# Block compression with its matmul sides swapped, in a one-core transformer kernel

## The chip, the cores and the metric

The kernel runs on one NeuronCore of a Trainium2 chip. The metric is the device time of one execution in microseconds (us). Three executions of the kernel before took 2712.67 to 2714.38 us, median 2713.49 us.

## The reference

The program is two transformer blocks over 512 positions of width 1024. The change touches one small part of the first block, the compression of keys and values for the sparse attention:

```python
def compress(kv, pe, w1, w2):
    """NSA compression phi: (B,S,G,hd) -> (B,Nc,G,hd); block i covers [i*STRIDE, i*STRIDE+CMP_BLOCK)."""
    ...
    blocks = blocks + pe[None, None, :, None, :]
    n_cmp = blocks.shape[1]
    flat = blocks.transpose(0, 1, 3, 2, 4).reshape(b, n_cmp, g, CMP_BLOCK * d)
    return jax.nn.silu(flat @ w1) @ w2

    k_cmp = rmsnorm(compress(kc, cmp_pe_k, cmp_w1_k, cmp_w2_k), k_norm_g)
    v_cmp = compress(vc, cmp_pe_v, cmp_w1_v, cmp_w2_v)
```

A block is 32 positions of 64 features, 2048 numbers; blocks start every 16 positions, so there are 31 of them for each of 4 groups, 124 in all. `w1` is 2048 x 256, `w2` is 256 x 64. It is done twice, for keys (q = 0) and for values (q = 1).

## The kernel before, in words

**Precision.** Nearly every product is made from numbers split in two: a high part rounded to `F32R` and the low rest. For a weight unit of 128 x 1024 numbers, ScalarE copies the high part (`split` in `act_program`, through `copy`, L1324), VectorE subtracts it from the raw weights (L1702), and TensorE makes three products, high x high, high x low, low x high (`three`, L870). All matmuls that are not transposes are recorded at L868.

**Order.** `order()` writes one list of items; each engine's program walks through that list and issues its share, so each engine's queue holds the items in the same order. Weight units are numbered as they are added; the split of unit n+1 is issued on ScalarE and VectorE just ahead of the item that uses unit n, into one of two buffers, and waits until TensorE has finished unit n-1. SyncE loads up to three units ahead.

**The stage.** `memory_branch` runs the attention over the memory (four heads of four tiles), and fills its waits with other work. `attend` (L279) adds for each tile a `score`, a `turn` of the tile three back, and two steps of the jobs. The jobs take turns: one is `wide` (L270), the queries of the next head: two dense units, then `widestat` (sum of squares by TensorE, then a chain of small VectorE and ScalarE operations, `rsqrt`, L1713), then `widefin` (TensorE spreads the result, VectorE scales both halves, ScalarE and VectorE split them). The next head's first `score` waits for that split. The other job is `compress()` (L402), then `queries` and `keys`.

**The compression.** `kvc` makes the projection (a dense unit), VectorE writes it to `C2`, feature by position, with the next position's features in the lower 64 partitions. `cmp(q, j)` handles weight unit j of 4 (four slabs of 128 x 256). Its weights are not split: `split=False`, the raw fp32 slab is the stationary side, in halves of 128 columns, and `C2` moves, 124 columns that lie 16 numbers (64 bytes) apart. A second matmul with one moving column adds the position encoding's part into another column of the bank. An fp32 matmul shows in the trace as two. After j = 3 VectorE copies that column to `hb` and ScalarE writes `hid` = silu(bank + hb), hidden unit by block, which `kc1` and `vc` multiply by `w2`.

Of the kernel before, what the change touches and what calls it, by code (L numbers as in the profile page):

```python
# [14 lines left out]
P = 128  # L15
# [200 lines left out]
def order():  # L216
# [461 lines left out]
def build(nc, A, out):  # L678
# [44 lines left out]
    hid = [place(f"hid{q}", 24576 + q * 256, 256).rearrange("p (t g c) -> p t g c", t=2, g=4) for q in range(2)]  # L723
    KX = place("KX", 25088, 128)
# [47 lines left out]
    hb = sb("hb", [P, 4])  # L772
# [90 lines left out]
    def pe_program(e):  # L863
# [230 lines left out]
        def cmp(q, j, n):  # L1094
            if j == 0:
                for ht in range(2):
                    take("d", ("cmp", q, ht), True)
                on.wait_ge(*evac.at(("c2", q, 1)))
            bs = [banks[("cmp", q, ht)] for ht in range(2)]
            on.wait_ge(*d_raw[n % NRAW].at(n))  # L1100
            for kk in range(4):
                kt = 4 * j + kk
                for ht in range(2):
# [4 lines left out]
            f.then_inc(*full.tick(("u", n), *([("cmp", q)] if j == 3 else [])))  # L1108
            if j == 3:
                for ht in range(2):  # L1110
                    banks.let_go(("cmp", q, ht))

        def kc1():
            b = take("d", ("kc1",))
            on.wait_ge(*d_w2.at(0))
            on.wait_ge(*curve.at(("hid", 0, 1)))
# [8 lines left out]
        def vc():  # L1125
            b = take("d", ("vc",))
            on.wait_ge(*curve.at(("hid", 1, 1)))
# [171 lines left out]
        def mmo(m, n):  # L1299
# [4 lines left out]
            for k in range(2):  # L1304
# [6 lines left out]
                  turn=turn, values=values, rel=rel, kvc=kvc, cmp=cmp, kc1=kc1, kc2=kc2, vc=vc, ng=ng, gn=gnt, sq=sq,  # L1311
# [8 lines left out]
    def act_program(e):  # L1320
# [143 lines left out]
        def cmp(q, j, n):  # L1464
            for ht in range(2 if j == 3 else 0):
                on.wait_ge(*evac.at(("hb", q, ht)))
                o = banks[("cmp", q, ht)][:, 0:124].rearrange("p (g c) -> p g c", g=4)
                on.wait_ge(*cleared.at("hid"))
# [972 lines left out]
```

## Time and profile before

| | us |
|---|---|
| median of three runs | 2713.49 |
| profiled execution | 2708.38 |
| its span, first to last instruction | 2706.6 |
| TensorE busy | 2544.7 (94%) |
| VectorE busy | 1350.9 (50%) |
| ScalarE busy | 1042.8 (39%) |
| mean granted TensorE clock | 0.963 of full |

Busy time is the time in which an engine has an instruction running. Loads of TensorE's stationary side (PEld) overlap its matmuls (PE). The names of buffers lose their numbers, so `C2` is `t_C` and `w_qm` units appear as `t_raw`, `t_whi`, `t_wlo`.

### The profile page before, as it was taken

Reading aid. Unit: us, or ns where it says so; the run is one execution under the profiler, and the core shown is the slowest. Engines: PE = TensorE matmul, PEld = TensorE weight load, DVE = VectorE, ACT = ScalarE, POOL = GpSimd, SP = SyncE. Lnnn points to the kernel's source line nnn. Section 1 sums busy time; section 2 is a strip of 40 time slices with the busy share of each in tenths; the row PEclk is TensorE's granted clock in tenths of the full one; section 3 lists DMA queues with packets and bytes.
Section 4 is the critical chain, followed back from the end, with each engine's and each line's share of the span. In section 5 each row is a group of like instructions: output and inputs, shape, how many; then the busy total and the mean of one; then the engine's idle time right before and its main releaser. Section 6 shows DMA issues by size and latency. Waiting matters only on the chain.

```text
span 2706.6 us, 31528 instructions
## 1 busy us (share of the span) xinstructions
PE 2544.7 (94%) x12154; PEld 2113.1 (78%) x12154; DVE 1350.9 (50%) x2707; ACT 1042.8 (39%) x1865; POOL 175.9 (6%) x236
## 2 busy tenths in 40 slices
PE   8989998899999999999999999999989988899998
PEld 6867887788788787877888887877878776688886
DVE  5424445433466656666543444655544455543444
ACT  4213334333454454444332233655542345322222
POOL 0000000000011111111000000111100002000000
PEclk9999998898899899999999999999989999999999
DMA  3473234122212111212223223211112331223222
GB/s 131 101 142 109 91 103 149 60 72 71 70 67 74 48 63 51 75 55 102 87 94 100 95 88 124 78 55 55 55 47 93 106 120 55 70 93 94 101 87 85
DMA packets 85982, 231.38 MB, mean 85 GB/s; under 512 B 8344, under 2 KB 23320, under 8 KB 85834
## 3 DMA queue, kind: packets, MB, share of 16 engines
q1 hardware_dynamic: 78480, 217.18, 24.1%
q10 hardware_dynamic: 7354, 12.19, 2.4%
q8 instruction: 98, 1.61, 0.3%
q14 instruction: 50, 0.41, 0.0%
HBM read 217.79 MB, written 11.53 MB: 85 GB/s over the span
## 4 chain that ended last, share of the span: by engine, by line
PE 81%; DVE 9%; ACT 5%; issue 2%; DMA 2%; POOL 1%; ACTq 1%; DVEq 0%; SPq 0%
PE bank L868 79%; DVE t_wlo L1702 2%; PE bank L1035 2%; DMA t_raw<-in_f_out 1%; ACT t_whi L1324 1%; DVE t_tmp L1774 1%; DVE t_ss L1903 0%; POOL t_pp L2257 0%; DVE t_CB L1774 0%; POOL t_pw L2259 0%; DVE t_tmp L1744 0%; ACT t_pp L1451 0%; DVE t_ST L2152 0%; ACTq L1392 0%; DVE t_tmp L1782 0%
## 5 line engine op out<-in xcount | busy, mean ns | idle before, releaser
L868 PE MATMUL bank<-t_XH,t_whi 128*128 128x512 f32 x2064 | 829.2, 402 | 53.8 <-DVE t_wlo L1702 24.8
L868 PE MATMUL bank<-t_XH,t_wlo 128*128 128x512 f32 x2064 | 815.8, 395 | 0.0
L868 PE MATMUL bank<-t_XL,t_whi 128*128 128x512 f32 x2064 | 815.6, 395 | 0.0
L1702 DVE TENSOR_TENSOR t_wlo<-t_raw,t_whi 128x1024 fp32r<-128x1024 f32 (+2 forms) x412 | 472.0, 1147 | 480.1 <-ACT t_whi L1324 475.2
L1324 ACT ACTIVATE t_whi<-t_raw 128x1024 fp32r<-128x1024 f32 (+2 forms) x412 | 407.2, 989 | 410.3 <-PE bank L868 361.9
L868 PEld LDWEIGHTS bank<-t_XH,t_whi 128*128 128x128 f32 x2064 | 396.2, 192 | 150.2 <-issue 42.3
L868 PEld LDWEIGHTS bank<-t_XH,t_wlo 128*128 128x128 f32 x2064 | 394.6, 191 | 85.1
L868 PEld LDWEIGHTS bank<-t_XL,t_whi 128*128 128x128 f32 x2064 | 395.7, 192 | 79.2
L868 PE MATMUL bank<-t_RX,t_whi 128*128 128x512 f32 x1056 | 334.1, 398 | 11.5 <-DVE t_wlo L1702 6.6
L868 PEld LDWEIGHTS bank<-t_RX,t_whi 128*128 128x128 f32 x1056 | 200.0, 190 | 60.5 <-ACT t_whi L1324 7.0
L1774 DVE TENSOR_TENSOR t_tmp<-bank,t_RB 128x512 f32<-128x512 f32 x170 | 117.0, 688 | 259.1 <-PE bank L868 256.1
L868 PE MATMUL bank<-t_RX,t_wlo 128*128 128x512 f32 x528 | 210.0, 398 | 0.0
L2259 POOL TENSOR_SCALAR t_pw<-t_pw,t_sa 128x256 f32<-128x256 f32 (+1 forms) x80 | 68.5, 859 | 984.8 <-DVE t_sa L1916 983.8
L1324 ACT ACTIVATE t_RX<-t_tmp 128x512 fp32r<-128x512 f32 x66 | 41.7, 632 | 223.6 <-DVE t_tmp L1782 223.6
L868 PEld LDWEIGHTS bank<-t_RX,t_wlo 128*128 128x128 f32 x528 | 99.9, 189 | 24.3
L2257 POOL TENSOR_SCALAR t_pp<-t_pp,t_sa,t_gn 128x128 f32<-128x128 f32 (+3 forms) x128 | 86.0, 672 | 412.4 <-DVE t_sa L1916 412.4
L1451 ACT ACTIVATE t_pp<-t_ss,t_sa 128x256 f32<-128x256 f32 (+3 forms) x144 | 79.8, 554 | 76.5 <-DVE t_sa L1903 74.9
L1385 ACT ACTIVATE t_tmp<-t_tmp 128x512 f32<-128x512 f32 x66 | 41.7, 632 | 133.9 <-DVE t_tmp L1774 133.9
L1035 PE MATMUL bank<-t_cst,t_pp 128*128 128x128 f32 x352 | 66.6, 287 | 19.9 <-POOL t_pp L2257 19.9
L1324 ACT ACTIVATE t_PS<-bank 128x128 fp32r<-128x128 f32 (+3 forms) x128 | 54.7, 427 | 79.0 <-PE bank L1035 78.7
L868 PE MATMUL bank<-t_OA,t_whi 128*128 128x512 f32 x256 | 81.9, 402 | 3.1 <-ACT t_OA L1324 3.1
L1324 ACT ACTIVATE t_XH<-t_XT,t_vec 128x512 fp32r<-128x512 f32 x48 | 34.6, 721 | 123.2 <-DVE t_XT L2078 57.9
(300 smaller groups left out, 2882.5 us busy)
## 6 DMA issues: line engine op xcount, KB each, us to landing
t_raw<-in_f_in SPq DMA_DIRECT2D x88, 512.0 KB, 3.2
t_raw<-in_f_out SPq DMA_DIRECT2D x32, 384.0 KB, 3.1
t_raw<-in_w_merge SPq DMA_DIRECT2D x24, 512.0 KB, 3.2
t_raw<-in_w_conv SPq DMA_DIRECT2D x24, 512.0 KB, 3.2
t_raw<-in_fg SPq DMA_DIRECT2D x22, 512.0 KB, 3.2
t_raw<-in_fu SPq DMA_DIRECT2D x22, 512.0 KB, 3.2
t_raw<-in_f_out SPq DMA_DIRECT2D x32, 320.0 KB, 2.9
t_raw<-in_w_g SPq DMA_DIRECT2D x16, 512.0 KB, 3.3
```

Of the source, the lines that this page charges most:

```text
L868: return e.matmul(o, l, r, start=start, stop=stop, skip_group_check=True)
L1035: f = e.transpose(b[:, j * P:(j + 1) * P], spare(hd, t)[1][:, j * P:(j + 1) * P], ident)
L1324: return e.activation(o, i, ACT.Copy, **how)
L1385: e.activation(s, a, ACT.Silu).then_inc(*curve.tick(("silu", f, h, m)))
L1451: e.activation(p[:, 0:wd], x[:, 0:wd], ACT.Exp, scale=-1.0, bias=s[:, 0:1], accum_out=s[:, 1:2]).then_inc(*curve.tick(("ex", t)))
L1702: e.tensor_tensor(wlo[n % NW][:, 0:width], raw[n % NRAW][:, 0:width], f32(whi[n % NW][:, 0:width]), ALU.subtract).then_inc(*w_lo.tick(n))
L1774: e.tensor_tensor(o, banks[item], RB, ALU.mult).then_inc(*evac.tick(done, ("free", item)))
L2257: e.tensor_scalar(p, p, r, gn[:, i, k:k + 1], ALU.mult, ALU.mult).then_inc(*scaled.tick(t))
L2259: e.tensor_scalar(p, p, r, None, ALU.mult).then_inc(*scaled.tick(t))
```

## The change

The sides of the compression's matmul are swapped, the position encoding is added before the matmul, and both sides are split.

- `cround(q, j)`, new, on VectorE: four `tensor_scalar` write the high part of C2's strided columns plus the position encoding, into `CH[0][j % 2]` (124 numbers wide, one for each of four slabs); then four `scalar_tensor_tensor` write the low part into `CH[1][j % 2]`.
- `cmp(q, j)` on TensorE: the 124 columns of `CH` are the stationary side, the split weights (256 columns, contiguous) move: 4 slabs x 3 products = 12 `F32R` matmuls, into one bank, block by hidden unit. Its unit is split as all others.
- ScalarE applies silu to the whole bank at once into `HS`; `hturn(q)`, new, turns `HS` back by two transposes on TensorE, and VectorE copies them to `hid`.
- `compress()` has one more step for each q: the first of them holds only a `cround`, and `cmp(q, 3)` stands by itself ahead of `hturn`. The copies to `hb` go.

```diff
             for j in range(4):
-                w.lin("cmp", q, j, name="cmp_w1", j=4 * q + j, split=False)
+                w.add("cround", q, j)
+                if j:
+                    w.lin("cmp", q, j - 1, name="cmp_w1", j=4 * q + j - 1)
                 yield
+            w.lin("cmp", q, 3, name="cmp_w1", j=4 * q + 3)
+            yield
+            w.add("hturn", q)
...
         def cmp(q, j, n):
...
-            for kk in range(4):
-                kt = 4 * j + kk
-                for ht in range(2):
-                    l = raw[n % NRAW][:, kk * 256 + ht * P:kk * 256 + (ht + 1) * P]
-                    o = bs[ht][:, 0:124].rearrange("p (g c) -> p g c", g=4)
-                    mm(o, l, C2[:, :, 2 * kt:2 * kt + 481:16], kt == 0, kt == 15)
-                    f = mm(bs[ht][:, 126:127], l, v(("pek", "pev")[q], kt), False, kt == 15)
+            b = take("d", ("cmp", q), True) if j == 0 else banks[("cmp", q)]
+            hi, lo = weights(n)
+            on.wait_ge(*x_lo.at(("cround", q, j)))
+            h, l = CH[0][j % 2], CH[1][j % 2]
+            for kk in range(4):
+                c = slice(kk * 256, (kk + 1) * 256)
+                f = three(b[0:124, 0:256], h[:, kk, 0:124], l[:, kk, 0:124], hi[:, c], lo[:, c],
+                          j == 0 and kk == 0, j == 3 and kk == 3)
...
+        def hturn(q):
+            b = take("d", ("hturn", q))
+            on.wait_ge(*curve.at(("hs", q)))
+            for ht in range(2):
+                f = e.transpose(b[:, ht * P:ht * P + 124], HS[0:124, ht * P:(ht + 1) * P], ident[0:124, 0:124])
+            f.then_inc(*full.tick(("hturn", q)))
...
         def cmp(q, j, n):
...
+            if j == 3:
+                on.wait_ge(*full.at(("cmp", q, 3)))
+                on.wait_ge(*full.at(("hturn", q - 1)))
+                e.activation(HS[0:124, :], banks[("cmp", q)][0:124, 0:256], ACT.Silu).then_inc(
+                    *curve.tick(("hs", q), ("free", ("cmp", q))))
...
+        def cround(q, j):
+            h, l = CH[0][j % 2], CH[1][j % 2]
+            on.wait_ge(*evac.at(("c2", q, 1)))
+            on.wait_ge(*full.at(("cmp", q, j - 2) if j > 1 else ("cmp", q - 1, j + 2)))
+            src = [C2[:, :, 2 * kt:2 * kt + 481:16] for kt in range(4 * j, 4 * j + 4)]
+            for kk in range(4):
+                o = h[:, kk, 0:124].rearrange("p (g c) -> p g c", g=4)
+                e.tensor_scalar(o, src[kk], v(("pek", "pev")[q], 4 * j + kk), None, ALU.add).then_inc(*calc.tick(("cround", q, j)))
+            on.wait_ge(*calc.at(("cround", q, j)))
+            for kk in range(4):
+                o, i = (x[:, kk, 0:124].rearrange("p (g c) -> p g c", g=4) for x in (l, h))
+                e.scalar_tensor_tensor(o, src[kk], v(("pek", "pev")[q], 4 * j + kk), f32(i), ALU.add, ALU.subtract).then_inc(
+                    *x_lo.tick(("cround", q, j)))
```

## Rows read from the trace of the kernel before

**Rows 1.** The profile page: TensorE, clock in 40 slices, chain by line.
```profile
PE 2544.7 (94%) x12154; PEld 2113.1 (78%) x12154; DVE 1350.9 (50%) x2707; ACT 1042.8 (39%) x1865; POOL 175.9 (6%) x236
...
PEclk9999998898899899999999999999989999999999
...
PE bank L868 79%; DVE t_wlo L1702 2%; PE bank L1035 2%; DMA t_raw<-in_f_out 1%; ACT t_whi L1324 1%; DVE t_tmp L1774 1%; DVE t_ss L1903 0%; POOL t_pp L2257 0%; DVE t_CB L1774 0%; POOL t_pw L2259 0%; DVE t_tmp L1744 0%; ACT t_pp L1451 0%; DVE t_ST L2152 0%; ACTq L1392 0%; DVE t_tmp L1782 0%
```

**Rows 2.** Windows, the eight compression blocks: busy by engine, clock, DMA share.
```profile
523.41:530.12 6.71, 6.71 (x35) 6.71 (x34) 1.17 (x7) 0.51 (x2) 0.00 (x0) 0.54 0.00 0
...
548.02:552.98 4.96, 4.96 (x34) 4.91 (x32) 1.23 (x1) 2.12 (x3) 0.00 (x0) 1.00 0.00 0
...
sum 44.21, PE 44.21 PEld 43.95 DVE 12.97 ACT 16.52 POOL 0.00; mean PE 5.53 PEld 5.49 DVE 1.62 ACT 2.06 POOL 0.00
```

**Rows 3.** Windows, the whole stage, then a slow and a fast stretch of one unit.
```profile
518.00:668.00 150.00, 141.60 (x704) 126.73 (x704) 53.39 (x122) 49.92 (x85) 10.51 (x12) 0.86 0.20 71
...
539.00:544.60 5.60, 5.60 (x19) 4.78 (x20) 1.45 (x5) 0.87 (x3) 0.92 (x1) 0.52 0.51 187
544.60:548.00 3.40, 3.40 (x16) 2.80 (x15) 0.00 (x0) 0.00 (x0) 0.00 (x0) 1.00 0.00 0
```

**Rows 4.** Waits of TensorE from 500 to 760 us: total, times, longest.
```profile
PE bank L868 <- DVE t_tmp L1843: 6.4, 3, 3.4
PE bank L868 <- DVE t_wlo L1702: 4.7, 5, 3.0
```

**Rows 5.** Timeline of TensorE: start, duration, instruction, idle before it.
```profile
506.20 0.88 PE L868 MATMUL bank<-t_MK,t_MQ 128*128 128x256 f32 x6
506.92 0.39 PE L868 MATMUL bank<-t_XH,t_whi 128*128 128x512 f32 x1
...
522.50 1.05 PE L868 MATMUL bank<-t_cst,t_tmp 128*128 128x1 f32 x8 [3.35 <-DVE t_tmp L1843]
...
531.96 1.91 PE L868 MATMUL bank<-t_cst,t_sn 128*128 128x128 f32 x8
...
539.00 1.63 PE L868 MATMUL bank<-t_MK,t_MQ 128*128 128x256 f32 x6
540.43 0.63 PE L1035 MATMUL bank<-t_cst,t_pp 128*128 128x128 f32 x2
540.71 0.78 PE L868 MATMUL bank<-t_XH,t_whi 128*128 128x512 f32 x1
...
567.12 1.05 PE L868 MATMUL bank<-t_cst,t_tmp 128*128 128x1 f32 x8 [1.53 <-DVE t_tmp L1843]
```

**Rows 6.** Timeline of VectorE.
```profile
525.04 0.16 DVE L1736 SCALAR_TENSOR_TENSOR t_sn<-t_sn,t_rn 128x4 f32<-128x4 f32 x1
...
533.91 0.69 DVE L1854 TENSOR_TENSOR t_wq<-t_wq,bank 128x512 f32<-128x512 f32 x1 [0.87 <-PE bank L868]
...
537.42 0.69 DVE L1707 TENSOR_TENSOR t_MQ<-t_wq,t_MQ 128x512 fp32r<-128x512 f32 x1 [0.77 <-ACT t_MQ L1324]
...
659.06 0.69 DVE L1822 SCALAR_TENSOR_TENSOR t_XT<-t_mg,bank 128x512 f32<-128x512 f32 x1 [0.68 <-PE bank L868]
```

**Rows 7.** Groups of VectorE, shapes apart: busy us, mean ns of one.
```profile
L1702 DVE TENSOR_TENSOR t_wlo<-t_raw,t_whi 128x1024 fp32r<-128x1024 f32 x316 | 386.5, 1224 | 340.7 <-ACT t_whi L1324 338.4
...
L1711 DVE SCALAR_TENSOR_TENSOR t_XL<-t_XT,t_vec,t_XH 128x512 fp32r<-128x512 f32 x48 | 36.0, 750 | 31.7 <-ACT t_XH L1324 31.7
...
L1707 DVE TENSOR_TENSOR t_PS<-bank,t_PS 128x128 fp32r<-128x128 f32 x32 | 8.7, 273 | 0.6 <-ACT t_PS L1324 0.4
...
L2039 DVE TENSOR_TENSOR t_tmp<-bank,t_TB 128x31 f32<-128x31 f32 x16 | 2.1, 195 | 0.0
...
L2039 DVE TENSOR_TENSOR t_tmp<-bank,t_TB 128x15 f32<-128x15 f32 x16 | 1.7, 169 | 0.0
```

**Rows 8.** Groups of ScalarE, shapes apart: the split of a unit.
```profile
L1324 ACT ACTIVATE t_whi<-t_raw 128x1024 fp32r<-128x1024 f32 x316 | 331.6, 1050 | 218.0 <-PE bank L868 201.4 <-issue 9.4 <-DMA t_raw<-in_f_in 4.5
```

**Rows 9.** Groups of TensorE's stationary loads, shapes apart.
```profile
L868 PEld LDWEIGHTS bank<-t_XH,t_whi 128*128 128x128 f32 x2064 | 396.2, 192 | 150.2 <-issue 42.3 <-DVE t_sa L1903 7.8 <-ACT t_whi L1324 7.7
```

More of the change, by code:

```diff
@@ L723, in build @@
     hid = [place(f"hid{q}", 24576 + q * 256, 256).rearrange("p (t g c) -> p t g c", t=2, g=4) for q in range(2)]
+    CH = [[place(f"CH{q}{d}", 25728 + 1024 * q + 512 * d, 512, F32R).rearrange("p (k n) -> p k n", k=4) for d in range(2)]
+          for q in range(2)]
+    HS = place("HS", 27776, 256)
     KX = place("KX", 25088, 128)
@@ L771, in build @@
     vch = sb("vch", [P, 64], F32R)
-    hb = sb("hb", [P, 4])
     csm = sb("csm", [P, 4, 4, 4])
@@ L1115, in kc1 @@
             on.wait_ge(*d_w2.at(0))
-            on.wait_ge(*curve.at(("hid", 0, 1)))
+            on.wait_ge(*evac.at(("hid", 0)))
             mm(b[:, 0:P], w2s[:, 0:P], hk[0], True, False)
@@ L1126, in vc @@
             b = take("d", ("vc",))
-            on.wait_ge(*curve.at(("hid", 1, 1)))
+            on.wait_ge(*evac.at(("hid", 1)))
             mm(b[:, 0:64], hk[2], w2s[:, 256:320], True, False)
@@ L1310, in pe_program @@
                   convg=convg, wide=wide, widestat=widestat, widefin=widefin, memv=memv, mgate=mgate, score=score,
-                  turn=turn, values=values, rel=rel, kvc=kvc, cmp=cmp, kc1=kc1, kc2=kc2, vc=vc, ng=ng, gn=gnt, sq=sq,
+                  turn=turn, values=values, rel=rel, kvc=kvc, cmp=cmp, hturn=hturn, kc1=kc1, kc2=kc2, vc=vc, ng=ng, gn=gnt, sq=sq,
                   sqstat=sqstat, sqfin=sqfin, sk=sk, skstat=skstat, skfin=skfin, sv=sv, cscore=cscore, cnorm=cnorm, cturn=cturn,
@@ L1464, in cmp @@
         def cmp(q, j, n):
[L1465 to L1468, printed above, removed]
-                e.activation(hid[q][:, ht, :, 0:31], o, ACT.Silu, bias=hb[:, 2 * q + ht:2 * q + ht + 1]).then_inc(
-                    *curve.tick(("hid", q, ht), ("free", ("cmp", q, ht))))
+            if j == 3:
[3 more added lines that the diff above has]
+                    *curve.tick(("hs", q), ("free", ("cmp", q))))
         def scaled_sq(b, sq, x, gain, sq_item, x_item, free):
@@ L1937, in kvc, with hturn @@
                     *evac.tick(("c2", q, x), ("free", ("kvc", q, x))))
-        def cmp(q, j, n):
-            if j == 3:
-                on.wait_ge(*full.at(("cmp", q)))
-                for ht in range(2):
-                    e.tensor_copy(hb[:, 2 * q + ht:2 * q + ht + 1], banks[("cmp", q, ht)][:, 126:127]).then_inc(
-                        *evac.tick(("hb", q, ht)))
+        def cround(q, j):
[11 more added lines that the diff above has]
+                    *x_lo.tick(("cround", q, j)))
+        def hturn(q):
+            on.wait_ge(*full.at(("hturn", q)))
+            on.wait_ge(*cleared.at("hid"))
+            src = banks[("hturn", q)][:, 0:256].rearrange("p (t n) -> p t n", t=2)
+            for ht in range(2):
+                e.tensor_copy(hid[q][:, ht, :, 0:31], src[:, ht, 0:124].rearrange("p (g c) -> p g c", g=4)).then_inc(
+                    *evac.tick(("hid", q), ("free", ("hturn", q))))
         def kc2():
@@ L2232, in dve_program @@
                   gateu=gateu, mmerge=mmerge, smerge=smerge, gmerge=gmerge, weigh=weigh, scale=scale, rest=rest,
-                  rel=rel, kvc=kvc, cmp=cmp, kc2=kc2, vc=vc, ng=ng, gn=gnt, sqstat=sqstat, sqfin=sqfin,
+                  rel=rel, kvc=kvc, cround=cround, hturn=hturn, kc2=kc2, vc=vc, ng=ng, gn=gnt, sqstat=sqstat, sqfin=sqfin,
                   skstat=skstat, skfin=skfin, skput=skput, svs=svs, csoft=csoft, cnorm=cnorm, cturn=cturn, msplit=msplit, po=po,
```

11 lines of the change are left out of this document (2 added, 9 removed).

## The prediction, before the run

> **What bounds the kernel now.** I read the page first. TensorE is busy 94% of the span, the chain that ended last lies on its matmuls for 79%, and the clock row dips below 9 in a few slices [rows 1]. So work taken off TensorE shortens the run, unless something it covered comes to light. The windows over the whole stage, 518 to 668 us, come next: TensorE 141.6 of 150 us, VectorE 53.4, ScalarE 49.9, mean clock 0.86 [rows 3]. VectorE has room on average; what counts is where its chains end. TensorE's waits say that: from 500 to 760 us it waits 6.4 us in three waits for the sum ahead of `widestat` (L1843) and 4.7 us for split weights [rows 4]. Everything else the small chains need is covered, and much of the cover is the compression.
>
> **What goes.** The windows over the eight `cmp` blocks: 4.96 us at full clock (1.00), up to 6.71 us where the clock is near its lower level of 1.2 GHz (0.54), 44.2 us in all, with TensorE busy throughout [rows 2]. The two pairs of copies to `hb` and the halves of the silu had their own short place beside other work; I put them at nothing either way, since silu, now one instruction, and its table loads stay.
>
> **What comes on TensorE.** Eight times 12 matmuls with 256 moving columns. The trace has six such (`score`): they start at 506.20 and the next matmul at 506.92, 0.12 us each; at the lower clock 539.00 to 540.43, 0.24 us each [rows 5]. A `cmp` block is then 1.44 us, or 2.86 us. TensorE's idle times ahead of `widestat` are what precede the slow stretches [rows 2, 3, 5], and three of the eight blocks follow such a wait at once; I take 3 x 2.86 + 5 x 1.44 = 15.8 us. Four transposes: two at the lower clock take 0.28 us (540.43 to 540.71) [rows 5], so about 0.6 us. Net work: 44.2 - 15.8 - 0.6 = 27.8 us less.
>
> The stationary side has 124 columns instead of 128. A stationary load lasts 192 ns [rows 9], longer than the 120 ns from one matmul to the next: the loads overlap, and I assume they go on doing so. If they didn't, a matmul would cost 0.19 us, 96 x 0.07 = 7 us more.
>
> **What comes on VectorE.** Eight splits more, 1.22 us each [rows 7], after 1.05 us on ScalarE [rows 8]: 9.8 and 8.4 us. Eight `cround` of eight instructions. Bounds for one instruction: from below 0.195 us (31 columns taken 16 apart); from above 0.75 us (the same kind of operation, 512 columns) [rows 7]. A contiguous 128 columns take 0.273 us. The strided reads cost (195 - 169)/16 = 1.6 ns a column, against (1224 - 273)/896 = 1.06 for contiguous ones, which puts 124 strided columns at 195 + 93 x 1.6 = 0.34 us [rows 7]. The writes here are contiguous and half the instructions have one tensor input. I take 0.31 us, 2.5 us for a `cround` (1.6 to 6.0), 20 us for the eight. The Trainium skill, SBUF — State Buffer, Door 1: The DMA port swizzle, says that SBUF has 16-byte lines and each access that crosses to a new line pays a penalty. The slope of 1.6 against 1.06 ns agrees; by contiguous rates alone a `cround` would be 2.2 us, and the sum below about 2 us better.
>
> VectorE in the stage goes from 53 to about 81 us, in some 136 us: still not the bound on average. DMA moves the same bytes and raw buffers come free sooner, after the split and not after the matmuls; nothing there.
>
> **Where the cover was.** This is the larger half of the working. I walked through the items. `compress()` gets two steps more, so everything behind its first `cround` moves: kvc(1,0) comes after `widefin` of head 2, kvc(1,1) goes beside the queries of head 3, cmp(1,2) and cmp(1,3) behind the values of head 1. Four places lose cover, with c = 2.5 for a `cround`:
>
> (a) Head 1's queries. Before: `widestat` at 522.50, cmp(0,0), `score`, `turn`, `widefin`, cmp(0,1), `score` at 539.00, the next dense unit at 540.71 [rows 5]. After: `widestat`, `score`, `turn`, `widefin`, cmp(0,0), `score`. The `rsqrt` chain ends at 525.2 [rows 6], so `widefin`, eight matmuls at the lower clock (531.96 to about 533.7 before [rows 5]), runs until 527.0. VectorE does `cround`(0,0) from 525.2 to 527.7: cmp(0,0) waits 0.7 and ends at 530.6. VectorE then has `weigh` and `rest` (about 1.0 us) and the query chain, which took 533.91 to 538.11 = 4.2 us [rows 6]: 532.9. `score` waits 2.3. Then on VectorE `cround`(0,1), 2.5, and the next unit's split, 1.2: 536.7, while TensorE has finished at 534.7: 2.0 more. Waits of 5.0 us, and the dense unit starts at 536.7 instead of 540.71.
>
> (b) `widestat` of head 2. Before it idled 1.53 us behind cmp(0,3) [rows 5]. With cmp(0,2) of 1.44 us and a split behind `cround`(0,3) ahead of the sum on VectorE, I get 2.5 us: 1.0 more.
>
> (c) Head 3's queries, where cmp(1,0) and cmp(1,1) cover less. Counting from `widestat`'s start: `widefin` at 5.6, VectorE has `cround`(1,1) and a split until 6.8, `weigh`, `rest` to 7.8, the query chain to 12.0, `cround`(1,2) and a split to 15.7. TensorE is ready for `score` at 8.6 to 10.0 and for the gate unit at 13.4: about 2.3 + 2.2 = 4.5.
>
> (d) cmp(1,3). The values of head 1 end at V; VectorE merges until V + 0.7 (it waited for them until 659.06, then 0.69 us [rows 6]), then `cround`(1,3) to V + 3.2 and the split to V + 4.4. cmp(1,2) is done at V + 1.4: 3.0 us. `hturn` is covered by `score` and `turn`.
>
> Together 13.5 us. Behind the stage, `sqfin` now stands after two gate units and loses a wait of under 1 us, while `skstat` loses its neighbours; I leave these at zero. Stretches at the lower clock outside the `cmp` blocks: 19 instructions in 5.60 us at 0.52 against 16 in 3.40 at 1.00 [rows 3] put one at about 1.6 us. The number of them seems the same after as before, with up to three more possible at the new waits; zero, with 5 us kept for the range.
>
> **The sum.** 27.8 - 13.5 = 14 us less. The profiled execution took 2708.38 us (span 2706.6 and 1.8 around it), so 2694.4; it lies 5.1 us below the median of the three runs, 2713.49. On that scale I predict **2699.5 us**, own range 2693 to 2706.
>
> **The rivals.**
>
> *Nearly all of the 27.8 us is kept.* `cround` is short (1.6 us) or the clock stays up. For it: VectorE is busy only 53 of 150 us. Against: it is the order of its queue, not its load, that makes the waits. At c = 1.6 six `cround` lie on the path of (a) to (d), 6 x 0.9 = 5.4 better, and with one slow stretch less 7: 2692.5; with no waits at all 2685.7. Chance 0.19.
>
> *The 124-column load is not hidden.* 0.19 us a matmul, 7 us more, 2706.5. For it: 192 ns against 120 [rows 9, 5]. Against: full-width loads of that length are hidden throughout, 2064 times. The Trainium skill, TensorE: Matmul & The Clock Gate, Weight-path perf modes, gives fast weight load only for 128 weights and no FP32; if `F32R` has it now, the change loses it, with the result of this case. Chance 0.10.
>
> *The waits eat it all.* The slow stretches multiply: each new wait of over 2 us, four of them, followed by a stretch that costs 1.6, plus (b) and the tail once more: 6 + 5 us, 2710.5. For it: before, the idle of 3.35 us was followed by a clock of 0.54 [rows 5, 2]. Chance 0.10.
>
> *VectorE decides, slower than before.* If strided instructions with two steps cost as much as 512 columns, 0.75 us, a `cround` is 6.0 us; the six on the path add 6 x 3.5 = 21: 14 - 21, 7 us slower, 2720.5. It turns at c = 2.5 + 14/6 = 4.8 us, 0.60 us an instruction. Against: 31 strided columns take 0.195 us. Chance 0.06.
>
> The forecast itself has 0.55.
>
> **How the numbers follow.** About 0.2% (5.4 us) can be told from no change here. The forecast and the first two rivals are all below 2708: 0.55 + 0.19 + 0.10 = 0.84 faster, less a little for their edges, 0.83. The third is half within 0.2%, and edges of others: 0.09 same. The rest, 0.08, slower. The range reaches from the first rival, 2687, to the third, 2710.
>
> **What would show each step.** `cmp` groups of 256 columns with starts 0.12 us apart; a wider spacing shows the load. `cround` groups near 0.31 us an instruction. TensorE's waits between 518 and 650 us: about 20 us in all, for t_MQ at the first `score` of heads 1 and 3, for t_wlo right behind it, for t_tmp (L1843) at `widestat`, for t_wlo at cmp(1,3). The gate unit of head 0 about 13 us earlier than before; the stage's mean clock not below 0.84. The prediction is wrong if these waits are under 8 or over 25 us, or if the gain appears outside the stage.

## The result and the profile after

The changed kernel takes 2698.43 us (median of four runs, 2693.39 to 2702.08); the kernel before, timed beside it, 2713.14. The ratio is 0.9946, 95% interval 0.9931 to 0.9962: 14.7 us faster, where 14 were forecast. Two later groups of runs gave 0.9953 (0.9934 to 0.9971) and 0.9949 (0.9929 to 0.9968). The profiled execution took 2702.08 us with a span of 2700.3; it is the slowest of its four, so its span understates the gain.

The page of the kernel after, its lines that answer to [rows 1]: 156 matmuls fewer, TensorE busy 27.9 us less, 31 us more on VectorE.

```profile
PE 2516.8 (93%) x11998; PEld 2082.8 (77%) x11998; DVE 1381.6 (51%) x2779; ACT 1051.0 (39%) x1870; POOL 176.5 (7%) x236
...
PEclk9999999898989999999999999999989999999999
...
PE bank L875 77%; DVE t_wlo L1709 2%; PE bank L1042 2%; ACT t_whi L1332 1%; DMA t_raw<-in_f_out 1%; DVE t_tmp L1781 1%; DVE t_ss L1910 1%; POOL t_pp L2279 0%; DVE t_CB L1781 0%; ACT t_pp L1459 0%; ACT t_tmp L1332 0%; POOL t_pw L2281 0%; DVE
```

Windows over three of the eight compression blocks, the answer to [rows 2]; all eight add up to 15.25 us of TensorE's time (forecast 15.8), where 44.21 stood. The number before the last two of a row is the granted clock: two of the eight blocks run at the lower clock (0.50), two more in part.

```profile
526.58:529.37 2.79, 2.79 (x13) 2.62 (x13) 2.02 (x7) 1.24 (x3) 0.92 (x1) 0.50 0.00 0
542.95:544.39 1.44, 1.44 (x13) 1.44 (x12) 0.00 (x0) 1.24 (x3) 0.00 (x0) 1.00 0.00 0
...
...
641.63:643.54 1.91, 1.91 (x13) 1.91 (x14) 1.03 (x1) 0.00 (x0) 0.00 (x0) 0.75 0.52 124
```

To compare the rest I cut both traces at the same items: from the first `score` of the memory attention (491.20 before, 490.00 after) to the first matmul of `kc1` (the product of `hid` with `w2`, the first item behind the compression), and from there to `sv`, the first weight unit of the values for the sparse attention. Between the two lie, among others, `skfin`, which spreads the norms of the sparse keys, and `skput`, which splits and stores them. The window views, before and then after; the third line of the second is the stretch of [rows 3].

```profile
491.20:664.30 173.10, 163.77 (x786) 144.43 (x787) 59.88 (x129) 56.65 (x93) 11.44 (x12) 0.87 0.20 70
664.30:741.80 77.50, 70.10 (x357) 57.63 (x355) 34.12 (x68) 36.75 (x58) 4.55 (x5) 0.89 0.16 55
```

```profile
490.00:651.30 161.30, 135.87 (x639) 115.07 (x639) 88.56 (x205) 63.94 (x101) 12.39 (x13) 0.88 0.22 72
651.30:727.80 76.50, 66.35 (x349) 54.84 (x347) 33.11 (x61) 31.99 (x51) 8.14 (x7) 0.91 0.23 76
518.00:668.00 150.00, 122.67 (x587) 104.70 (x588) 86.86 (x210) 65.16 (x106) 13.31 (x14) 0.87 0.21 71
```

In the first stretch, the stage from here on, TensorE is busy 163.77 us before and 135.87 after: 27.9 less. It is idle 9.3 us before and 161.30 - 135.87 = 25.4 after: 16.1 more. The stage is 11.8 us shorter. In the second stretch the idle time goes from 7.4 to 10.2, the busy time falls by 3.8, and 1.0 us more is gained.

The waits of TensorE from 500 to 760 us, against [rows 4], and the timeline of TensorE with the idle time ahead of each, against [rows 5]:

```profile
PE bank L875 <- DVE t_wlo L1709: 17.6, 9, 3.2
PE bank L875 <- DVE t_tmp L1850: 8.8, 3, 3.3
PE bank L875 <- DVE t_sn L1743: 4.8, 2, 4.3
PE bank L875 <- DVE t_MQ L1714: 3.8, 3, 1.5
```

```profile
521.32 1.05 PE L875 MATMUL bank<-t_cst,t_tmp 128*128 128x1 f32 x8 [3.35 <-DVE t_tmp L1850]
...
531.42 0.59 PE L875 MATMUL bank<-t_MK,t_MQ 128*128 128x256 f32 x3 [1.20 <-DVE t_MQ L1714]
...
534.95 0.77 PE L875 MATMUL bank<-t_XH,t_whi 128*128 128x512 f32 x1 [2.71 <-DVE t_wlo L1709]
...
546.68 0.47 PE L875 MATMUL bank<-t_XH,t_whi 128*128 128x512 f32 x1 [1.19 <-DVE t_wlo L1709]
...
557.41 1.86 PE L875 MATMUL bank<-t_cst,t_tmp 128*128 128x1 f32 x8 [2.63 <-DVE t_tmp L1850]
...
606.73 1.05 PE L875 MATMUL bank<-t_cst,t_tmp 128*128 128x1 f32 x8 [2.84 <-DVE t_tmp L1850]
...
621.52 0.77 PE L875 MATMUL bank<-t_XH,t_whi 128*128 128x512 f32 x1 [2.72 <-DVE t_wlo L1709]
...
641.63 0.35 PE L875 MATMUL bank<-t_whi,t_CH 128*124 128x256 f32 x1 [2.92 <-DVE t_wlo L1709]
...
724.19 3.68 PE L875 MATMUL bank<-t_cst,t_sn 128*64 128x128 f32 x32 [4.29 <-DVE t_sn L1743]
...
737.00 0.36 PE L875 MATMUL bank<-t_whi,t_XH 128*128 128x256 f32 x1 [3.15 <-DVE t_wlo L1709]
```

The place names of the prediction are, in this order: `widestat` of head 1; (a) the second half of head 1's queries and the dense unit behind them; a dense unit two items later; (b) `widestat` of head 2; `widestat` of head 3; (c) the gate unit (a dense weight unit for the output gate) behind head 3's queries; (d) cmp(1,3). The last two lie behind the stage: `skfin`, and the second `sv` unit.

### The profile page after: what moved, and what is told of

Read it like the earlier page. It is cut to its first block, busy times and chain, and to the rows that moved or that the text cites. A ratio compares the mean times of both kernels' runs of the same rounds, so it can differ in the third digit from the quotient of the medians.

```text
span 2700.3 us, 31304 instructions
## 1 busy us (share of the span) xinstructions
PE 2516.8 (93%) x11998; PEld 2082.8 (77%) x11998; DVE 1381.6 (51%) x2779; ACT 1051.0 (39%) x1870; POOL 176.5 (7%) x236
## 4 chain that ended last, share of the span: by engine, by line
PE 78%; DVE 10%; ACT 6%; issue 3%; DMA 2%; POOL 1%; ACTq 1%; DVEq 0%; SPq 0%
PE bank L875 77%; DVE t_wlo L1709 2%; PE bank L1042 2%; ACT t_whi L1332 1%; DMA t_raw<-in_f_out 1%; DVE t_tmp L1781 1%; DVE t_ss L1910 1%; POOL t_pp L2279 0%; DVE t_CB L1781 0%; ACT t_pp L1459 0%; ACT t_tmp L1332 0%; POOL t_pw L2281 0%; DVE t_tmp L1751 0%; DVE t_ST L2174 0%; ACTq L1400 0%
## 5 line engine op out<-in xcount | busy, mean ns | idle before, releaser
L1709 DVE TENSOR_TENSOR t_wlo<-t_raw,t_whi 128x1024 fp32r<-128x1024 f32 (+2 forms) x420 | 482.0, 1149 | 480.7 <-ACT t_whi L1332 476.1
L1332 ACT ACTIVATE t_whi<-t_raw 128x1024 fp32r<-128x1024 f32 (+2 forms) x420 | 416.1, 992 | 409.5 <-PE bank L875 360.8
L875 PE MATMUL bank<-t_RX,t_whi 128*128 128x512 f32 x1056 | 333.8, 397 | 11.8 <-DVE t_wlo L1709 6.9
```

The lines of the kernel that those rows point to most:

```text
L875: return e.matmul(o, l, r, start=start, stop=stop, skip_group_check=True)
L1332: return e.activation(o, i, ACT.Copy, **how)
L1709: e.tensor_tensor(wlo[n % NW][:, 0:width], raw[n % NRAW][:, 0:width], f32(whi[n % NW][:, 0:width]), ALU.subtract).then_inc(*w_lo.tick(n))
```

## The experiments

Times are medians; each ratio is to the kernel before on the same chip, with its 95% interval. The kernel before ran at 2708.86 us in the first group (30 runs, 2700.27 to 2719.05), 2713.03 in the second and 2711.65 in the third. "Stage" is the stretch from the first `score` to `kc1`, "first values" the time from the first `score` to the first matmul with the sparse values; both are read in one profiled execution, to about 0.1 us. Three profiles of the changed kernel (after, e0_again, e11_control) differ by 1.3 us in the stage and by 2.9 us at the first values, so smaller differences of single profiles say nothing. Where runs of different groups are compared, go by the ratios.

| | median us | ratio | stage | first values |
|---|---|---|---|---|
| before (profile) | 2713.14 | 1 | 173.1 | 287.1 |
| after | 2698.43 | 0.9946 | 161.3 | 280.0 |
| e0_again | 2692.91 | 0.9953 [0.9934, 0.9971] | 162.2 | 278.4 |
| e1_order_only | 2718.90 | 1.0035 [1.0019, 1.0051] | 173.1 | 290.9 |
| e2_old_steps | 2703.85 | 0.9976 [0.9961, 0.9991] | 162.2 | 279.7 |
| e3_round_twice | 2716.48 | 1.0035 [1.0021, 1.0049] | 178.4 | 297.2 |
| e4_swap | 2693.22 | 0.9942 [0.9923, 0.9960] | 158.6 | 274.7 |
| e5_pairs | 2702.80 | 0.9969 [0.9956, 0.9983] | (other order) | 284.2 |
| e6_few_rounds | 2691.87 | 0.9924 [0.9910, 0.9939] | 155.1 | 271.1 |
| e7_high_on_act | 2694.41 | 0.9940 [0.9925, 0.9955] | 157.5 | 276.2 |
| e8_zero_later | 2692.52 | 0.9930 [0.9909, 0.9951] | 158.2 | 273.4 |
| e9_early_third | 2688.85 | 0.9915 [0.9894, 0.9936] | 153.5 | 271.2 |
| e10_both | 2687.09 | 0.9914 [0.9892, 0.9935] | 153.6 | 270.4 |
| e11_control | 2697.01 | 0.9949 [0.9929, 0.9968] | 161.0 | 277.1 |

**e0_again**, the changed kernel once more, as the measure for the first group.

> The changed kernel once more, with five rounds. Theory (the gain is 28 to 29 us of matmuls less, minus about 15 us of waits that appear where the compression was the cover): 12 to 16 us below the kernel before. It also shows how far its executions spread; the first four went from 2693.4 to 2702.1, and if that is the clock's state at the waits, a second profile should show the same waits in the stage and a different length behind it.

0.9953; its waits lie where those of the first profile lie (`widestat` 3.36, 2.63 and 2.85, units 2.73, 1.20 and 2.44, cmp(1,3) 2.94). The places are a property of the order, not of one execution.

**e1_order_only**, the kernel before with the item order of the change and nothing else:

```diff
             for j in range(4):
-                w.lin("cmp", q, j, name="cmp_w1", j=4 * q + j, split=False)
+                if j:
+                    w.lin("cmp", q, j - 1, name="cmp_w1", j=4 * q + j - 1, split=False)
                 yield
+            w.lin("cmp", q, 3, name="cmp_w1", j=4 * q + 3, split=False)
+            yield
```

> The kernel before with nothing but the new order of steps (two more steps, each cmp one step later; raw weights, old matmuls). Theory: the order itself costs, behind the stage, where the norms of the queries and keys lose their neighbours (in the changed kernel TensorE waits 4.3 us for the key statistics and 3.2 us for the split of the second value unit, which the kernel before did not): 3 to 6 us slower than before, with the stage itself about as long. Rival A: the order is free (within 2 us) and those waits come from the rounding and the splits on VectorE. Rival B: the order gains, because compression blocks now lie beside other chains: faster by over 2 us.

The order alone makes the kernel 0.35% slower. The stage is not the cause (173.1 us, as before); the loss stands behind it. Timeline of TensorE in e1_order_only, `skfin` and the second `sv` unit:

```profile
738.65 3.68 PE L871 MATMUL bank<-t_cst,t_sn 128*64 128x128 f32 x32 [4.28 <-DVE t_sn L1739]
...
751.47 0.35 PE L871 MATMUL bank<-t_whi,t_XH 128*128 128x256 f32 x1 [2.68 <-DVE t_wlo L1705]
```

Before, these two waits were 1.92 and 0.58 us. The same pair, 4.29 and 3.15, stands in the changed kernel. So the two extra steps cost the tail about 4 us whatever the compression does. Its median lies farther off than its trace says, and outside the 3 to 6 us that were expected: 10 us slower by the median, 3.8 by the trace at the first values. More on this below.

**e2_old_steps**, the change with the old number of steps: `cround`(q,0) goes into the step of kvc(q,1), and `cround`(q,j+1) follows cmp(q,j).

```diff
                 w.lin("kvc", q, x, name="w_kvc", j=2 * q + x)
+                if x:
+                    w.add("cround", q, 0)
                 yield
             for j in range(4):
-                w.add("cround", q, j)
-                if j:
-                    w.lin("cmp", q, j - 1, name="cmp_w1", j=4 * q + j - 1)
+                w.lin("cmp", q, j, name="cmp_w1", j=4 * q + j)
+                if j < 3:
+                    w.add("cround", q, j + 1)
                 yield
-            w.lin("cmp", q, 3, name="cmp_w1", j=4 * q + 3)
-            yield
```

> The changed kernel with the number of steps of before: the first rounding of each half right behind its projection, every other one in the step ahead of its matmuls, so that no item behind the compression moves. Theory: the waits of 4.3 and 3.2 us behind the stage go back to what they were before (about 4 us better), while widestat of head 1 waits for one rounding more (2.4 us): 2694 to 2700, about 0 to 4 us better than the changed kernel. Rival: the order doesn't matter and VectorE's rounding ahead of widestat is added on top: 2 to 4 us slower than the changed kernel.

The tail is as before again (`skfin` waits 1.93 us, `sv` 0.60). But the rounding now stands ahead of `widestat`'s sum: 5.85 us at head 1 and 4.89 at head 3, and silu's result is waited for (1.65 and 0.82 us). Stage 162.2 us, the same as with the new order. The expectation was missed: in place of 0 to 4 us better, the whole program is 0.23 percentage points (6 us) worse than e0_again, though the two intervals overlap. In the traces the old order saves the two waits of the tail and has TensorE idle 3 us longer in the stage (28.9 us against 25.9); they don't show why it comes out slower in all.

**e3_round_twice**: every `cround` is done two times over.

```diff
+            for _ in range(2):
                 for kk in range(4):
...
+                on.wait_ge(*x_lo.at(("cround", q, j)))
```

> The changed kernel with every rounding done twice over (8 instructions more for each of 8, about 2.45 us each, 19.6 us more on VectorE; the result is the same). Theory: what counts is where a rounding lies in VectorE's queue; five or six of the eight are ahead of a chain that TensorE waits for, so 12 to 16 us slower than the changed kernel, about level with the kernel before. Rival 1: VectorE has room (58% busy in the stage), so under 6 us slower. Rival 2: every rounding counts in full: 19 us or more slower.

23.6 us slower than e0_again by the medians. Windows of the stage in e0_again and in e3_round_twice:

```profile
487.20:649.40 162.20, 136.34 (x638) 115.61 (x639) 88.50 (x205) 63.91 (x101) 12.40 (x13) 0.87 0.22 72
```

```profile
486.40:664.80 178.40, 139.44 (x639) 117.85 (x640) 108.84 (x269) 63.90 (x101) 12.39 (x13) 0.84 0.20 66
```

TensorE is idle 25.9 us in the one and 39.0 in the other: 13.1 more, for eight roundings of 2.4 us each (19 us). By the idle time some five and a half of the eight lie on the path; the prediction counted six. The clock falls with it, from 0.87 to 0.84, and TensorE is busy 3.1 us longer. The time came out above the 12 to 16 us that were expected, in the range of the second rival (19 us or more), so the idle time of the stage is not the whole price; the first values come 18.8 us later, the rest was not located. With a `cround` of twice the cost (4.8 us) the change is a loss of 9 us (1.0035), where the prediction's sum has its turn: it undercounts what a longer rounding costs.

**e4_swap**: in each step the matmuls' item stands ahead of the rounding.

```diff
             for j in range(4):
-                w.add("cround", q, j)
                 if j:
                     w.lin("cmp", q, j - 1, name="cmp_w1", j=4 * q + j - 1)
+                w.add("cround", q, j)
                 yield
```

> The changed kernel with the two lines of a step swapped: the block's matmul unit is added first and the next rounding after it, so that in VectorE's queue the split of the next dense unit goes ahead of the rounding. Theory (the waits are a matter of what stands ahead of what in VectorE's queue): the two waits of 2.7 us for split weights, at the dense unit behind the first score of head 1 and at the gate unit of head 2, nearly go, nothing else moves: 4 to 6 us faster than the changed kernel, 0.65 to 0.7% faster than the kernel before. Rival (VectorE's or the clock's total is what counts): no difference.

```profile
529.97 0.47 PE L875 MATMUL bank<-t_XH,t_whi 128*128 128x512 f32 x1 [0.60 <-DVE t_wlo L1709]
...
553.91 1.86 PE L875 MATMUL bank<-t_cst,t_tmp 128*128 128x1 f32 x8 [4.88 <-DVE t_tmp L1850]
...
615.99 0.77 PE L875 MATMUL bank<-t_XH,t_whi 128*128 128x512 f32 x1 [0.60 <-DVE t_wlo L1709]
...
635.87 0.36 PE L875 MATMUL bank<-t_whi,t_CH 128*124 128x256 f32 x1 [2.96 <-DVE t_CH L1957]
```

The two units behind `score` now wait 0.60 us, where they waited 2.71 and 2.72: their split no longer stands behind a rounding in VectorE's queue. `widestat` of head 2 pays: 4.88 against 2.63, now that `cround`(0,3) is just ahead of its sum. cmp(1,3) is unchanged, only the name of what it waits for is another (t_CH, not t_wlo). The two waits went as expected, but "nothing else moves" was wrong, and so were the 4 to 6 us: the stage is 2.7 us shorter, and by the ratio the two kernels can't be told apart.

**e5_pairs**: two roundings in one step, then two compression blocks in one step.

```diff
-            for j in range(4):
-                w.add("cround", q, j)
-                if j:
-                    w.lin("cmp", q, j - 1, name="cmp_w1", j=4 * q + j - 1)
+            w.add("cround", q, 0)
+            w.add("cround", q, 1)
+            yield
+            for j in (0, 2):
+                w.lin("cmp", q, j, name="cmp_w1", j=4 * q + j)
+                w.lin("cmp", q, j + 1, name="cmp_w1", j=4 * q + j + 1)
+                if j == 0:
+                    w.add("cround", q, 2)
+                    w.add("cround", q, 3)
                 yield
-            w.lin("cmp", q, 3, name="cmp_w1", j=4 * q + 3)
-            yield
```

> The changed kernel with its compression in pairs: two roundings in one step, then two matmul blocks (and the next two roundings), then two blocks; three steps for each half instead of five, so that dense units come sooner and a step's cover is 2.9 us. Theory: fewer places where a 1.4 us block is the only cover; the query chains of heads 1 and 3 are covered by a pair or a dense unit; but two roundings in a row (4.9 us) stand ahead of one chain, and the second block of a pair waits for its split: between 6 us faster and 2 us slower than the changed kernel. Rival (order costs only behind the stage): as much faster as the order alone was slower with the old matmuls, 4 to 9 us.

The tail is like before's (`skfin` 1.65), but the second block of a pair now waits for ScalarE's split of its own unit: 2.07 or 2.08 us three times, and once 5.72. A block of 1.44 us can't cover a split chain of 1.05 + 1.22 us. Fewer steps are no gain: 0.9969, by the ratios 4 to 6 us slower than the changed kernel, outside the range that was expected.

**e6_few_rounds**: only the first two of each four roundings are done (`cround`(q,2) and (q,3) return at once), so the third and fourth blocks read the halves of the first and second.

```diff
-            on.wait_ge(*x_lo.at(("cround", q, j)))
+            on.wait_ge(*x_lo.at(("cround", q, j % 2)))
...
             src = [C2[:, :, 2 * kt:2 * kt + 481:16] for kt in range(4 * j, 4 * j + 4)]
+            if j > 1:
+                return
```

> The changed kernel with four of the eight roundings left out (j = 2 and 3 of both halves; their matmuls use the numbers of j = 0 and 1): 9.8 us less on VectorE. Theory: of these four, two lie on the path, the one ahead of the gate unit of head 2 and the one ahead of the last block; the two of the first half do not, since VectorE idled behind them: 4 to 6 us faster than the changed kernel. Rival (every rounding counts in full, as the 22 us for eight doubled ones could mean): 9 to 11 us faster.

```profile
560.41 1.87 PE L875 MATMUL bank<-t_cst,t_tmp 128*128 128x1 f32 x8 [2.63 <-DVE t_tmp L1850]
...
622.38 0.76 PE L875 MATMUL bank<-t_XH,t_whi 128*128 128x512 f32 x1 [0.60 <-DVE t_wlo L1709]
...
639.59 0.35 PE L875 MATMUL bank<-t_whi,t_CH 128*124 128x256 f32 x1 [0.58 <-DVE t_wlo L1709]
```

The gate unit waits 0.60 us in place of 2.72, cmp(1,3) 0.58 in place of 2.92. `widestat` of head 2 still waits 2.63 us, though the rounding ahead of it is gone: the prediction's cause for (b) is wrong. Four roundings fewer shorten the stage by 7.1 us (162.2 to 155.1), of which these two waits are 4.5. By the ratios the gain over the changed kernel is 6 to 8 us, between the theory's 4 to 6 and the rival's 9 to 11.

**e7_high_on_act**: e4_swap, and ScalarE writes the high half (`Identity` with the encoding as bias), VectorE only the low one.

```diff
+                e.activation(o, C2[:, :, 2 * kt:2 * kt + 481:16], ACT.Identity, bias=v(("pek", "pev")[q], kt)).then_inc(
+                    *x_hi.tick(("cround", q, j)))
...
-                e.tensor_scalar(o, src[kk], v(("pek", "pev")[q], 4 * j + kk), None, ALU.add).then_inc(*calc.tick(("cround", q, j)))
-            on.wait_ge(*calc.at(("cround", q, j)))
+            on.wait_ge(*x_hi.at(("cround", q, j)))
```

> As the kernel with the swapped lines, and the high halves of the roundings on ScalarE (an activation with the position encoding as bias), the low ones stay on VectorE: VectorE's part of a rounding falls from 2.45 to about 1.4 us, ScalarE gets about 1.5 us each. Theory: 2 to 4 us faster than the swapped one, since the rounding no longer delays the query chain of head 1 and the sums so much. Rival: ScalarE, in whose queue the rounding now stands ahead of the exponentials and splits, gives it back: no faster.

No difference to e4_swap, as the rival said: cmp(1,3) waits 1.89 in place of 2.96, but `widestat` of head 3 waits 4.93 in place of 2.83. Half the rounding is off VectorE, and the other half now waits for ScalarE: ahead of that `widestat` VectorE idles 3.11 us for the high half, which ScalarE begins at 603.51, behind two reads of a dense unit's result that could not start before 602.45. The work moved, and the waits with it.

**e8_zero_later**: e4_swap, and GpSimd's memsets wait for a later event.

```diff
         def sparsezero():
-            on.wait_ge(*full.at(("values", 3)))
+            on.wait_ge(*full.at(("skfin", 0, 1)))
```

> e4_swap, but GpSimd's memsets of `sparsezero` wait for the second `skfin` of the keys in place of the values of head 3. Theory (the 2.53 us of the tensor_scalar L1730 are VectorE held up by GpSimd's 4.37 us memset of t_VS beside it): the instruction takes 0.17 us again, TensorE's wait for t_sn ahead of `skfin` falls from 4.28 to about 1.9 us, and the time is about 2.4 us below e4_swap; VectorE's subtractions in `skput`, which now meet the memset, may be held up in their turn, up to 4 us, without TensorE waiting for them. Rival (the 2.53 us come from the place of the item in VectorE's queue, not from GpSimd): L1730 stays at 2.53 us and the wait at 4.28.

For the instruction and the wait, as the theory expected. In the changed kernel, GpSimd and VectorE, timelines; the tensor_scalar of 16 numbers ends, at 722.68, when the memset does, at 722.66:

```profile
718.29 4.37 POOL L2291 MEMSET t_VS<- 128x5120 f32 x1 [40.14 <-PE bank L875]
```

```profile
720.15 2.53 DVE L1730 TENSOR_SCALAR t_sn<-t_sn 128x16 f32<-128x16 f32 x1
```

In e8_zero_later (GpSimd, VectorE, TensorE) the memset starts at 720.21, and the same instruction takes 0.17 us; `skfin` waits 1.92 us. By the ratios (0.9930 and 0.9942, of different groups) the time is some 3 us below e4_swap, where 2.4 were expected, but the intervals overlap for the most part: the gain in time is not shown. The first values come 1.3 us earlier, less than profiles of one kernel differ.

```profile
720.21 4.38 POOL L2291 MEMSET t_VS<- 128x5120 f32 x1 [49.00 <-PE bank L875]
```

```profile
714.83 0.17 DVE L1730 TENSOR_SCALAR t_sn<-t_sn 128x16 f32<-128x16 f32 x1
...
719.98 2.84 DVE L2037 TENSOR_TENSOR t_KS<-t_tmp 64x512 fp32r<-64x512 f32 x4 [0.77 <-ACT t_tmp L1332]
```

```profile
716.51 3.62 PE L875 MATMUL bank<-t_cst,t_sn 128*64 128x128 f32 x32 [1.92 <-DVE t_sn L1743]
```

**e9_early_third**: e4_swap, and `cround`(q,3) follows `cround`(q,2) at once.

```diff
-                w.add("cround", q, j)
+                if j < 3:
+                    w.add("cround", q, j)
+                if j == 2:
+                    w.add("cround", q, 3)
```

> e4_swap, but `cround`(q,3) is issued in the step before, right behind `cround`(q,2), so the step of cmp(q,2) holds no rounding. Theory (each wait is the rounding that happens to stand ahead of a small chain in VectorE's queue): in e4_swap `widestat` of head 2 waits 4.88 us and cmp(1,3) 2.96 us for `cround`(q,3); these fall to about 2.6 and 0.6 us, 4 to 5 us less than e4_swap, unless the doubled rounding (5 us on VectorE) shows up ahead of the unit or the queries that follow it, which would give 2 to 3 us of that back. Rival (the waits are the price of the new item order itself, whichever rounding stands where): they stay at 4.9 and 3.0 us and the time is that of e4_swap.

```profile
548.42 0.35 PE L878 MATMUL bank<-t_whi,t_CH 128*124 128x256 f32 x1 [2.32 <-issue]
...
552.56 1.05 PE L878 MATMUL bank<-t_cst,t_tmp 128*128 128x1 f32 x8 [1.53 <-DVE t_tmp L1853]
...
631.77 0.35 PE L878 MATMUL bank<-t_whi,t_CH 128*124 128x256 f32 x1 [0.53 <-issue]
```

`widestat` of head 2 waits 1.53 us as before the change, and cmp(1,3) 0.53. What the expectation named as the danger came in part: cmp(0,2) waits 2.32 us, put down to "issue", but VectorE's split of its unit, behind the two roundings, ends at that moment (547.10 + 1.22 = 548.32). The two waits together (3.85 us) are longer than the 2.63 us of the changed kernel at this place. The stage is 5.1 us shorter than in e4_swap, 7.5 shorter than in e11_control. In time it is 0.9915; the upper end of its interval, 0.9936, just overlaps the lower end of the control's, 0.9929.

**e10_both**: the two edits together.

> Both edits, of e8_zero_later and e9_early_third, on e4_swap. If the two act in separate places, the gains add: 6 to 7 us below e4_swap, about 0.9% below the kernel before. If the time is governed by the clock's slow stretches rather than by the waits, it is within 2 us of e4_swap.

0.9914: 9.9 us under the control by the medians. The trace shows both effects (`skfin` 1.92, cmp(1,3) 0.53), and the first values come 4.3 us earlier than in e4_swap. It is the fastest median of all, but by the intervals it can't be told from e9_early_third alone (0.9915): the later memset adds nothing to the time that these runs can show. The upper end of its interval, 0.9935, just overlaps the lower end of the control's, 0.9929.

**e11_control**: the changed kernel on the chip of the third group.

> The changed kernel once more, on this chip, as the measure for the other three: ratio 0.994 to 0.996 to the kernel before; e4_swap is at most 3 us below it by the waits counted in their traces (2.1 us less at each of the two units behind `score`, 2.3 us more at `widestat` of head 2).

0.9949; e4_swap's 0.9942, of the second group, is 2 us under it, within what was expected and within the intervals.

## Why the prediction was right, step by step

*TensorE's work: right.* The net was 27.8 us; the windows show 27.9. The matmuls start 0.12 us apart at the full clock. The timeline of TensorE over cmp(0,1), its first matmul and the one behind its last:

```profile
542.95 0.28 PE L875 MATMUL bank<-t_whi,t_CH 128*124 128x256 f32 x1
...
544.39 0.28 PE L875 MATMUL bank<-t_MK,t_MQ 128*128 128x256 f32 x1
```

(544.39 - 542.95)/12 = 0.12. Three blocks were put at the lower clock; two were, and two more in part, which comes to the same.

The change does several things at once: it swaps the sides, folds in the encoding and splits both sides. No run takes these apart. Rows of the kernel before say something of it. Both of these stretches have the full clock; the first is in cmp(0,2), the second is `kc1`, whose moving side is fp32 too, 128 columns that lie together:

```profile
548.59 0.65 PE L868 MATMUL bank<-t_C,t_raw 128*128 128x124 f32 x2
549.06 0.29 PE L868 MATMUL bank<-t_vec,t_raw 128*128 128x1 f32 x2
...
664.31 0.61 PE L868 MATMUL bank<-t_hid,t_w2s 128*128 128x128 f32 x4
664.75 0.56 PE L868 MATMUL bank<-t_w2s,t_hid 128*128 128x64 f32 x4
```

The 124 columns 64 bytes apart take 0.47 us for the two recorded instructions, the 128 that lie together 0.22 ((664.75 - 664.31)/2), and the one column of the encoding another 0.16. By these rows I estimate that a block of eight fp32 matmuls with a contiguous moving side and the encoding already added would take 8 x 0.22 = 1.8 us against the 1.44 of the changed kernel, with no split of its weights. That rival was not built, nor is the stride shown by a run of its own to be the cause, so what share of the gain is the swap's and the split's is open.

*The load of 124 columns: no cost.* At 0.12 us a matmul there is nothing of the 0.19 that the rival asked for, and in the same block a load takes 0.18 to 0.19 us (before, with 128 columns, 0.192). That rival, and the rule of the Trainium skill (TensorE: Matmul & The Clock Gate, Weight-path perf modes) by which the narrower load would lose its speed, would have shown here; the trace shows no such difference.

*`cround`: right within 5%.* Groups of VectorE with shapes apart (busy us, mean ns of one), and its timeline: one rounding, the split behind the next one, and the split ahead of `widestat` of head 2:

```profile
L1957 DVE SCALAR_TENSOR_TENSOR t_CH<-t_C,t_vec,t_CH 128x124 fp32r<-128x124 f32 x32 | 11.4, 418 | 0.3
...
L1953 DVE TENSOR_SCALAR t_CH<-t_C,t_vec 128x124 fp32r<-128x124 f32 x32 | 8.3, 327 | 0.0
```

```profile
523.95 1.03 DVE L1953 TENSOR_SCALAR t_CH<-t_C,t_vec 128x124 fp32r<-128x124 f32 x4
...
525.02 1.41 DVE L1957 SCALAR_TENSOR_TENSOR t_CH<-t_C,t_vec,t_CH 128x124 fp32r<-128x124 f32 x4
...
533.59 1.21 DVE L1709 TENSOR_TENSOR t_wlo<-t_raw,t_whi 128x1024 fp32r<-128x1024 f32 x1
...
554.60 1.23 DVE L1709 TENSOR_TENSOR t_wlo<-t_raw,t_whi 128x1024 fp32r<-128x1024 f32 x1 [2.43 <-ACT t_whi L1332]
```

The mean of one is 327 and 418 ns, but they overlap: four and four fill 523.95 to 526.35, 2.40 us, 0.30 an instruction where 0.31 was taken. The slope of the strided groups [rows 7] had given 0.34, and the step down to 0.31 was a guess that came out. The 2.2 us by contiguous rates are not far from 2.40 either, and no run has a contiguous `cround`, so what the stride costs here isn't tested. VectorE's load in the stage had been added up wrongly: 53 + 9.8 + 20 is 83 us, not 81; nothing else rests on it.

*The waits in the stage: right in kind, 2.6 us short.* 13.5 us more were counted, 16.1 came. Between 518 and 650 us TensorE is idle 23.7 us, where about 20 were forecast and over 25 would have made the prediction wrong. The gate unit of head 0 starts 13.5 us earlier (571.25 against 584.76), forecast 13.
- (a) 5.0 forecast; 0.41 + 1.20 + 2.71 = 4.3 came, and the dense unit starts 13.6 us behind `widestat`, forecast 14.2. For the 2.71 the cause is the one named: the rounding begins at 531.20, and the split can start only behind it, at 533.59, and ends at 534.80; e4_swap, which takes it out of there, waits 0.60.
- (b) 2.5 forecast, 2.63 came, for another reason. VectorE had idled 2.43 us for ScalarE's half when it began its split at 554.60; e6_few_rounds has the same wait without the rounding. By these rows it is the split chain of the unit, which a block of 1.44 us no longer covers, where one of 4.96 did.
- Missed for the same reason: `widestat` of head 3 (2.84, before 1.53) and a dense unit (1.19, before none). Together 2.5 us, about what the count lacked; the other differences nearly cancel. I had followed the roundings through VectorE's queue, but not the added splits through ScalarE's.
- (c) 4.5 forecast; 0.42 + 1.17 + 1.47 + 2.72 = 5.8 came.
- (d) 3.0 forecast, 2.92 came. e6_few_rounds and e9_early_third confirm the rounding as its cause.
- The rest is small: 0.52 us more ahead of `widefin` of head 1 and 0.2 at a dense unit, against 1.3 us in three waits of before that are gone.

*The tail at zero: wrong.* The gain was 11.8 us at `kc1`, 12.8 at the first `sv`, and 7.1 at the first sparse values. `skstat` "loses its neighbours" was written down and priced at nothing; it cost 4.29 - 1.92 = 2.4 us at `skfin` and 3.15 - 0.58 = 2.6 at `sv`. Between `sv` and the first values TensorE is also busy 39.1 us at a clock of 0.92, before 35.9 us at 1.00. That isn't the wait alone: e2_old_steps, which has the short wait, shows 39.2 us at 0.91 there. The first is GpSimd's memset (e8_zero_later). The second stands in e8 too (3.26); ahead of that split ScalarE has the 2.60 us of `skput` that used to have `values` and a gate unit beside it. That the order makes this wait is shown by e1_order_only (2.68) and e2_old_steps (0.60); the way it does so I only argued.

*Where the sum closes, and where it doesn't.* By the profiles of e0_again and e11_control the first values come 8.7 and 10.0 us earlier than before, by the medians the program is 16.0 and 14.6 us faster. No stretch of the profiles shows the other 5 us. Ahead of the first `score` and behind the first values all kernels do the same work (some 2008 and 8773 matmuls in every trace), and the fourteen profiles took 486.4 to 492.7 us for the one and 1922.5 to 1934.7 us for the other; the kernel before, with 491.2 and 1928.3, lies inside both. So single profiles differ by more in work that is the same than what is sought. The whole program's clock goes with the time from run to run: of the 30 runs of the kernel before in the first group one took 2719.05 us at a granted clock of 0.959 and one 2700.27 at 0.966. The changed kernel's runs have a median clock of 0.966, those of before 0.961 to 0.963, and those of e1_order_only 0.959, with a profile (2709.51 us) that is its fastest run. Whether the clock follows from the change is not shown: behind the first values it is 0.97 in the profiles of before, after, e0_again and e11_control alike. So the median came out as forecast partly by luck: the waits cost 2.6 us more than counted and those of the tail some 5 us, the stretch that the change touches became 7.1 to 10.0 us shorter in the profiles and not 14, and a gain of 5 us or more, which the forecast had at zero, lies where no stretch shows it. By the prediction's own sign ("if the gain appears outside the stage") this part of it failed: the stage has 10.9 to 12.1 us of the gain.

*The rivals.* Nearly all kept: no, 16 us of waits. The load: no. Slow stretches eat it: no; the clock from 518 to 668 us is 0.87, above the 0.84 that was set as the floor. VectorE decides: not at 0.30 us an instruction, but e3_round_twice, at twice that, is already 9 us slower than the kernel before, where the rival had the break-even.

## What to carry to other kernels

Where a matmul block shrinks from 5 us to 1.4, list what it covered on every engine's queue, the splits on ScalarE as well as the new work on VectorE; 16.1 of the 27.9 us saved went back into waits, which the busy shares of the engines did not show and a walk through the queues showed for the most part. Put new work in a queue where no short chain stands behind it: moving a few lines of the order (e9_early_third, 0.9915 beside the control's 0.9949) brought, by the medians, 8 us more on top of the change's 15, with intervals that just overlap. A change of order reaches past the stage that it is made for, so its tail has to be costed, item by item, too. And before two sides are swapped, look at what the slow side costs by itself: here the strided moving side took 0.47 us where a contiguous one of the same kind took 0.22.

## What the hardware showed that was not expected

A small tensor_scalar on VectorE (128 x 16, one input and one output in SBUF) was held for 2.53 us, against 0.17, until GpSimd's memset of 128 x 5120 ended. The wait of 4.28 or 4.29 us that follows from it stands in each kernel whose order puts the two side by side; with another order (e2_old_steps, e5_pairs) or a later memset (e8_zero_later, e10_both) it is 1.65 to 1.93. The Trainium skill, GPSIMD Engine Reference, Specifications, says that GpSimd shares its SBUF interfaces with VectorE, and names instructions in a 2-port mode or with two SBUF inputs as those that contend. For the tensor_scalar, which has one SBUF input, the trace agrees if it ran in a 2-port mode, which the trace doesn't show. Two SBUF inputs cost nothing beside this memset, which by its row reads no tensor; no run here has them beside a GpSimd instruction that does: in the kernel before, four subtractions of 64 x 512 take 2.84 us from 743.41, the first two beside the memset that starts at 740.94 and ends at 745.31, and the same 2.84 us in e8_zero_later, beside it at 719.98, and in the changed kernel from 731.99, with GpSimd idle.

```profile
740.94 4.37 POOL L2269 MEMSET t_VS<- 128x5120 f32 x1 [42.90 <-PE bank L868]
```

```profile
721.87 0.17 DVE L1723 TENSOR_SCALAR t_sn<-t_sn 128x16 f32<-128x16 f32 x1
...
743.41 2.84 DVE L2015 TENSOR_TENSOR t_KS<-t_tmp 64x512 fp32r<-64x512 f32 x4 [0.78 <-ACT t_tmp L1324]
```
